# Decode compression of an NSA layer by three products for each pair of compressed rows, with the turning banks emptied by ScalarE

## The chip, the cores and the metric

One Trainium2 chip, one of its cores. The metric is the device time of one execution in microseconds, the median of three runs. All data is fp32.

## The reference, cut to what matters

One decoder layer mixes an HGRN2 head group and an NSA head group, for a prompt of 512 positions and for one new token of each of 8 samples, each with 4096 past positions in 32 pages of 128. For a sample the NSA group computes from its past rows (4 key-value heads of 64 columns):

```
compress(rows, w1, w2, pe), kind k (keys) and v (values):
    sub[n]  = rows[16 n : 16 n + 16]                        # 256 sub-blocks of 16 rows
    h[n]    = const + sub[n] . w1[first half] + sub[n+1] . w1[second half]    # 128 hidden columns
    out[n]  = silu(h[n]) . w2                               # 255 compressed rows
cmp_attention over the 255 compressed rows -> o_cmp and probabilities p
select_blocks(p): the 16 blocks of 64 rows with the highest score (3 of them forced)
selected_attention over the chosen 1024 rows; window_attention over the last 512 rows
out = g0 * o_cmp + g1 * o_slc + g2 * o_win, then the output projection and LayerNorm
```

## The kernel before, in words

hgrn_phase and middle_phase (0 to 1149 us) do the input projection, the HGRN2 group and the whole prompt. decode_output_phase does the decode compression and attention of the 8 samples, then the output projection for all rows (16 tiles of 16 products) and the LayerNorm. The change lies in this last phase, with small edits of the index tables in middle_phase.

**Compression.** GpSimd gathers compressed rows' inputs from the paged cache with indirect DMAs of 128 indices of 2 KB (`rows`, L1481) into X[half], one half of a sample's sub-blocks each (Xr0, and X1, which lies in the old xT): 16 for a half, 32 for a sample. A pass is a pair of kind (keys, values) and half; a sample has four passes. TensorE turns the pass's data (`turn`, L1527, 8 units of four 128x128 transposes into one of two PSUM banks dtb), VectorE empties one half of a bank and ScalarE the other (`empty`, L1754 and L1755, 64x512 each) into XT, and 16 products of 128x128 with 512 columns (`product`, L1550) sum up in one PSUM bank dpH. A pass's turns are made during the pass before it. At a pass's end ScalarE takes the sigmoid (L1804), VectorE the product with it (L1874), and `second` multiplies by w2 into dpK.

**Attention** is cut into pieces, each put by the table PIECES (LAST for the last sample) at a position (g, n) of the passes; `program` makes every engine walk through passes and positions in the same written order, so that an engine that waits in a piece holds back all that stands behind it. The pieces of compressed attention end with the indices gi (L1972) of the chosen rows. Then GpSimd gathers these in four quarters of 8 indirect DMAs (`chosen`, L1497) into the single buffer KV; a quarter is gathered only when the one before has been copied out: `fetch` lets ScalarE copy the keys to Kc (L1830) and VectorE the values to Vg (L1981), `keys` turns Kc (L1650), and so on to the scores, the window's rows and the sum. In GpSimd's own program the gathers of 8 compressed rows for the next sample and a quarter of chosen rows for the sample before alternate:

```
            for p in range(NB + 1):
                for q in range(4):
                    if p + 1 < NB:
                        rows(p + 1, 1 - q // 2, q % 2)
                    if p:
                        chosen(p - 1, q)
```

The passes run on for 9 output tiles (`output`, L1564), so that the last samples' attention lies beside output products. SP loads the window rows and, when X1 and Xr0 are free, the output weights (4 MB each, L1422), then x and the LayerNorm vectors.

## Time and profile before

| | us |
|---|---|
| three runs | 2365.11, 2371.79, 2372.05; median 2371.79 |
| span of the profiled execution, first to last instruction | 2102.9 |
| its own device time | not listed; median less span is 268.9 |
| busy: TensorE / its weight loads | 2062.7 (98%) / 1398.8 (67%) |
| busy: VectorE / ScalarE / GpSimd | 887.5 (42%) / 578.9 (28%) / 628.5 (30%) |

The span is what the hardware profiler saw of the program; the runs' device time has the launch around it. A matmul of fp32 operands appears as two records, a transpose as one. Busy time of DMA-issuing instructions counts on GpSimd (DMA_INDIRECT), where the engine itself makes the descriptors. "idle before" is the engine's idle time just ahead of an instruction, with who ended it; "issue" is idle time for which the profile shows no wait.

### The profile page before, as it was taken

To read this page: it belongs to the slowest core of one execution; us is meant where nothing else is said; L and a number is where in the kernel's file an instruction comes from. 1 tells how busy PE (TensorE), PEld (TensorE's weight loads), DVE (VectorE), ACT (ScalarE), POOL (GpSimd) and SP (SyncE) were. 2 spreads that over 40 slices of the span, in tenths; PEclk is the share of its full clock that TensorE was granted. 3 is DMA by queue.
4 is the path that set the end of the run, shared out by engine and by line. 5 is a ranking of instruction groups with operands and counts; after the bars stand their busy time and mean duration, and the time that the engine had idled before them with its cause. 6 is when DMAs were issued, how large, how long until landed. Compare 5 with 4: busy or idle time off the path is not lost. (4 is left out here: it accounts for less than half of the span.)

```text
span 2102.9 us, 24612 instructions
## 1 busy us (share of the span) xinstructions
PE 2062.7 (98%) x9559; PEld 1398.8 (67%) x9559; DVE 887.5 (42%) x1772; ACT 578.9 (28%) x1067; POOL 628.5 (30%) x675
## 2 busy tenths in 40 slices
PE   8999999999999999999998999999999999899997
PEld 7888888888888887777775555455554555344442
DVE  0354545454531014444445354554545545231227
ACT  0231133113310002322333333434444344200013
POOL 0000000000002003343434537776766765342000
PEclk9999999999999999999998999999999999999998
DMA  5222212222222221111114535566565665643224
GB/s 198 90 80 91 91 71 80 91 91 71 80 82 102 100 87 56 58 43 41 41 41 108 184 112 156 163 192 187 166 197 150 199 195 183 248 129 145 82 80 161
DMA packets 69104, 248.33 MB, mean 118 GB/s; under 512 B 11300, under 2 KB 28912, under 8 KB 57360
## 3 DMA queue, kind: packets, MB, share of 16 engines
q1 hardware_dynamic: 35480, 136.44, 18.6%
q0 software_dynamic: 32256, 106.46, 17.0%
q10 hardware_dynamic: 1280, 4.23, 0.5%
q8 instruction: 59, 0.97, 0.2%
q14 instruction: 29, 0.24, 0.0%
HBM read 226.46 MB, written 20.63 MB: 117 GB/s over the span
## 5 line engine op out<-in xcount | busy, mean ns | idle before, releaser
L292 PE MATMUL pj<-xT,strips 128*128 128x260 f32 x2368 | 532.9, 384 | 6.6 <-DMA xT<-d_xT 6.6
L1550 PE MATMUL dpH<-XT,w 128*128 128x512 f32 x1024 | 505.4, 604 | 0.7 <-DVE XT L1754 0.7
L292 PEld LDWEIGHTS pj<-xT,strips 128*128 128x128 f32 x2368 | 446.2, 191 | 72.5 <-issue 6.6
L1497 POOL DMA_INDIRECT KV<-d_cache,gi x256 | 245.3, 958 | 201.3 <-issue 70.7
L792 PE MATMUL pj<-xT,strips 128*128 128x260 f32 x1216 | 291.0, 387 | 0.0
L792 PEld LDWEIGHTS pj<-xT,strips 128*128 128x128 f32 x1216 | 222.0, 190 | 59.1 <-issue 29.6
L1550 PEld LDWEIGHTS dpH<-XT,w 128*128 128x128 f32 x1024 | 168.2, 190 | 115.7 <-issue 112.5
L1754 DVE COPY XT<-dtb 64x512 f32<-64x512 f32 x256 | 174.8, 683 | 140.2 <-PE dtb L1527 138.7
L1755 ACT ACTIVATE XT<-dtb 64x512 f32<-64x512 f32 x256 | 152.7, 596 | 217.6 <-PE dtb L1527 217.2
L1018 POOL MEMSET kbd<- 128x128 f32 x1 | 0.2, 204 | 635.9 <-POOLq L126 635.9
L1044 POOL TENSOR_SCALAR old<-old,rd 128x128 f32<-128x128 f32 (+3 forms) x116 | 121.9, 1066 | 166.9 <-DVE rd L1153 166.9
L1481 POOL DMA_INDIRECT Xr<-d_cache,row x128 | 121.0, 945 | 53.7 <-issue 38.3
L1481 POOL DMA_INDIRECT xT<-d_cache,row x112 | 106.0, 947 | 51.0 <-issue 33.8
L1564 PE MATMUL dpH<-xT,oT 128*128 128x512 f32 x256 | 118.5, 613 | 0.0
L1564 PE MATMUL dpH<-Xr,oT 128*128 128x512 f32 x256 | 113.1, 596 | 0.0
L1527 PEld LDWEIGHTS dtb<-const,Xr 128*128 128x128 f32 x512 | 62.9, 141 | 70.6 <-issue 59.6
L1527 PEld LDWEIGHTS dtb<-const,xT 128*128 128x128 f32 x512 | 64.7, 143 | 67.0 <-issue 65.4
L1564 PEld LDWEIGHTS dpH<-Xr,oT 128*128 128x128 f32 x256 | 47.6, 190 | 59.8 <-issue 59.6
L1564 PEld LDWEIGHTS dpH<-xT,oT 128*128 128x128 f32 x256 | 48.0, 194 | 56.5 <-issue 56.2
L1170 DVE COPY PT<-mpT 128x512 f32<-128x512 f32 (+2 forms) x48 | 28.9, 602 | 125.3 <-PE mpT L880 125.2
L1527 PE MATMUL dtb<-const,xT 128*128 128x128 f32 x512 | 78.1, 277 | 2.4 <-PEq L126 1.8
L988 ACT ACTIVATE PT<-mpT 128x512 f32<-128x512 f32 (+2 forms) x48 | 25.2, 525 | 199.0 <-PE mpT L880 199.0
(299 smaller groups left out, 2176.6 us busy)
## 6 DMA issues: line engine op xcount, KB each, us to landing
strips<-d_w_in SPq DMA_DIRECT2D x60, 1024.0 KB, 5.1
xT<-d_w_out SPq DMA_DIRECT2D x4, 4096.0 KB, 13.9
d_win_sample<-Wt SPq DMA_DIRECT2D x8, 1024.0 KB, 6.7
Xr<-d_w_out SPq DMA_DIRECT2D x2, 4096.0 KB, 14.6
Wt<-d_win SPq DMA_DIRECT2D x8, 896.0 KB
xT<-d_xT SPq DMA_DIRECT2D x8, 520.0 KB, 9.4
Sold<-d_state SPq DMA_DIRECT2D x8, 512.0 KB, 5.4
vB<-v_rows ACTq DMA_DIRECT2D x8, 512.0 KB, 6.9
```

What stands on the lines that cost most here:

```text
L292: mm = nc.tensor.matmul(pj[b][:, a, 0:TH], w[b][:, k, :], xT[:, k, a * TH:(a + 1) * TH], start=(k == 0), stop=(k == KT - 1))
L792: mm = nc.tensor.matmul(bank(s)[:, n, 0:TH], w[s % 2][:, k, :], xT[:, k, n * TH:(n + 1) * TH], start=(k == 0), stop=(k == KT - 1))
L988: nc.scalar.activation(blocks(brs, 0, qt), pT[:, 0:len(brs) * (qt + 1) * P].rearrange("p (r c n) -> p r c n", r=len(brs), n=P), ACT.Copy). ...
L1044: ins = nc.gpsimd.tensor_scalar(p, p, rd[U % 4][:, k:k + 1], None, ALU.mult)
L1170: V.tensor_copy(blocks(brs, 1, qt), pT[:, 0:len(brs) * (qt + 1) * P].rearrange("p (r c n) -> p r c n", r=len(brs), n=P)).then_inc(pe_v, 1)
L1481: pool.indirect_dma_start(out=X[half][:, r, :], out_offset=None, in_=pairs, in_offset=bass.IndirectOffsetOnAxis(ap=row[:, 2 * b + half, r: ...
L1497: pool.indirect_dma_start(out=KV[0:n, t - 2 * q, h, :], out_offset=None, in_=heads, in_offset=bass.IndirectOffsetOnAxis(ap=gi[b % 2][0:n, ...
L1527: mm = nc.tensor.transpose(tb[bank][:, j * P:(j + 1) * P], X[half][:, 2 * (4 * jg + j) + a, (2 * k + hp) * P:(2 * k + hp + 1) * P], ident)
L1550: mm = nc.tensor.matmul(pH[g % 2][:], w1[:, g % 2, n, :], XT[g % 2][:, jp, :, r:r + HSUB], start=(n == 0), stop=(n == NS - 1))
L1564: mm = nc.tensor.matmul(pH[i % 2][:], oT[:, k, t * P:(t + 1) * P], wo[c % 2][:, k, :], start=(k == 0), stop=(k == KT - 1))
L1754: copy = (lambda d, s: nc.vector.tensor_copy(d, s)) if par == 0 else (lambda d, s: nc.scalar.activation(d, s, ACT.Copy))
L1755: lambda d, s: nc.scalar.activation(d, s, ACT.Copy))
```

## The change

Compressed rows are taken in pairs. With E and O the even and odd sub-blocks, W0 and W1 the two halves of w1: the even output is O.(W0+W1) + (E-O).W0, the odd one O.(W0+W1) + (E'-O).W1, where E' is the next even sub-block. The three products have 512 columns each (128 pairs, 4 heads), so 24 for a kind and 48 for a sample in place of 64. W0+W1 is computed once into ws. To have E and O apart, the index tables gather sub-blocks by parity (X[par]), in quarters of 4 indirect DMAs each (q, of 16 row positions).

The order of work is now counted in slots, one product each: 3 for a step (two of the 32 row positions of w1), 24 for a kind, 48 for a sample. In six slots stand four units of turning (one Q): unit u0 in slot 6Q-7, u1 to u3 in the next three. ScalarE empties each unit's bank with two copies of 64x512 into O and E (Or, D2); VectorE makes E-O and E'-O behind u3 (D1 and D2, four TENSOR_TENSOR of 128x512 for a Q). There are three PSUM banks for the sums; ScalarE copies the common sum to SBUF (`keep_sum`), VectorE adds it to the other two (`join_sum`), then sigmoid (`bend`) and product (`finish`). All banks of keys and window rows that were turned are emptied by VectorE. The tables AT and LAST give the pieces' slots (counted from the sample's first slot); the piece `mix` is what `values` did on TensorE. GpSimd's program now takes all gathers of compressed rows of the next sample, then all four quarters of chosen rows of this one. The output weights are loaded in quarters. The code of `chosen`, and of most attention pieces, is unchanged.

```diff
-        XT = [sb(f"XT{n}", [P, CD // 2, KVH, HSUB + 1]) for n in range(2)]
+        big = sb("big", [P, 16, 512])
+        Or, D1, D2 = (big[:, a:a + 4] for a in (0, 4, 8))
+        ws = big[:, 12:16].rearrange("p a n -> p (a n)").rearrange("p (k j e) -> p k j e", k=2, j=NJ)
...
+        sg = Kc[:].rearrange("p t h d -> p (t h d)")
...
-        pH = [ps(f"dpH{n}", [P, 512]) for n in range(2)]
-        pK, pO = ps("dpK", [P, 512]), ps("dpO", [P, 512])
+        pH = [ps(f"dpH{n}", [P, 512]) for n in range(3)]
+        pK = ps("dpK", [P, 512])
         pS = ps("dpS", [P, 1024])
+        pO = pS[:, 512:768]
...
+        AT = {
+            ("second", 0): 27, ("second", 1): 29, "queries": 25, "scores": 31, "weights": 34, "turned": 36,
+            "sums": 37, "first": 38, "values": 39, "slots": 40, "bases": 41, "rows": 45,
+            ("second", 2): 51, ("second", 3): 53, "fetch0": 54, "keys0": 55, "mix": 56, "acc": 57,
+            "fetch1": 63, "keys1": 64, "fetch2": 70, "keys2": 71, "fetch3": 80, "keys3": 81,
+            "SCORES": 94, "SCALE": 96, "TURNED": 98, "VALUES": 100, "NEWEST0": 106, "NEWEST1": 108,
+            "WSCORES": 109, "WSCALE": 113, "WTURNED": 115, "WVALUES": 116, "SUM": 117, "DONE": 122,
         }
...
+        LAST = {
+            "SCORES": 83, "SCALE": 85, "TURNED": 87, "VALUES": 89, "NEWEST0": 90, "NEWEST1": 91,
+            "WSCORES": 93, "WSCALE": 95, "WTURNED": 97, "WVALUES": 98, "SUM": 99, "DONE": 103,
         }
...
+        UNITS = (1, 0), (1, 1), (0, 0), (0, 1)
...
+        def unit(t):
+            s, n = divmod(t, 3)
+            if s % 2 == 1 and n == 2:
+                Q, u = (s + 3) // 2, 0
+            elif s % 2 == 0:
+                Q, u = s // 2 + 1, n + 1
+            else:
+                return None
+            return (Q, u) if Q < NSTEP // 2 else None
...
+            for s in range(NSTEP):
+                for n in range(3):
+                    do["product"](s, n)
+                    then = unit(3 * s + n)
+                    if then:
+                        do["turn"](*then)
+                    name, which = pieces.get(3 * s + n, (None, None))
+                    if name in do:
+                        do[name](which)
+            for u in range(KT * TILES):
+                i, k = divmod(u, KT)
+                do["output"](i, k)
+                name, which = pieces.get(3 * NSTEP + u, (None, None))
+                if name in do:
+                    do[name](which)
+                if k == KT - 1:
+                    do["end"](i)
...
-                sp.dma_start(wo[n][:], io["w_out"][c]).then_inc(wo_in[n], 16)
-            def read(b, g):
-                for u in (6, 7):
-                    bank, k = place[(g, b, u)]
-                    sp.wait_ge(tr[bank], k + 1)
-            for b in range(NB - 2):
+                for a in range(4):
+                    if i < 2:
+                        bank, k = place[NSTEP // 2 - 4 + a, 1 + 2 * n]
+                        sp.wait_ge(tr[bank], k + 1)
+                    sp.dma_start(wo[n][:, 4 * a:4 * a + 4], io["w_out"][c][:, 4 * a:4 * a + 4]).then_inc(wo_in[n][a], 16)
+            for b in range(NB - 1):
                 window(b)
-            read(NB - 1, 1)
             weights(0)
-            window(NB - 2)
-            read(NB - 1, 3)
             weights(1)
-            for n in range(2):
-                sp.wait_ge(hid[n], 2 * NB)
+            sp.wait_ge(prod, NSTEP)
+            sp.wait_ge(hs_r, 4 * NB)
             for t in range(NQT):
                 sp.dma_start(z[t], io["x"][t * P:(t + 1) * P]).then_inc(z_in, 16)
...
-            def rows(b, half, part):
-                if b and part == 0:
-                    for u in (6, 7):
-                        bank, k = place[(3 - 2 * half, b - 1, u)]
-                        pool.wait_ge(tr[bank], k + 1)
-                for r in range(8 * part, 8 * part + 8):
+            def rows(b, q, par):
+                if b:
+                    bank, k = place[NJ * b - 4 + q, 3 - 2 * par]
+                    pool.wait_ge(tr[bank], k + 1)
+                for r in range(4 * q, 4 * q + 4):
                     pool.indirect_dma_start(
-                        out=X[half][:, r, :], out_offset=None, in_=pairs,
-                        in_offset=bass.IndirectOffsetOnAxis(ap=row[:, 2 * b + half, r:r + 1], axis=0),
-                    ).then_inc(x_in[half][part], 16)
+                        out=X[par][:, r, :], out_offset=None, in_=pairs,
+                        in_offset=bass.IndirectOffsetOnAxis(ap=row[:, 2 * b + par, r:r + 1], axis=0),
+                    ).then_inc(x_in[par][q], 16)
...
-            rows(0, 0, 0)
-            rows(0, 0, 1)
-            for p in range(NB + 1):
+            for q in range(4):
+                rows(0, q, 0)
+            for p in range(NB):
+                if p + 1 < NB:
+                    for q in range(4):
+                        rows(p + 1, q, 1)
+                        rows(p + 1, q, 0)
                 for q in range(4):
-                    if p + 1 < NB:
-                        rows(p + 1, 1 - q // 2, q % 2)
-                    if p:
...
-            def turn(g, b, u):
-                k, half = g % 2, half_of(g)
-                a, hp, jg = u % 2, u // 2 % 2, u // 4
-                if u % 4 == 0:
-                    pe.wait_ge(x_in[half][jg], 128 * b + 128)
-                bank = free((g, b, u))
-                for j in range(4):
-                    mm = nc.tensor.transpose(tb[bank][:, j * P:(j + 1) * P],
-                                             X[half][:, 2 * (4 * jg + j) + a, (2 * k + hp) * P:(2 * k + hp + 1) * P],
-                                             ident)
+            def turn(Q, u):
+                m, q = divmod(Q, 4)
+                b, kind = divmod(m, 2)
+                par, a = UNITS[u]
+                if kind == 0 and a == 0:
+                    pe.wait_ge(x_in[par][q], 64 * (b + 1))
+                bank = free((Q, u))
+                for i in range(4):
+                    r, hp = 4 * q + 2 * (i // 2) + a, i % 2
+                    mm = nc.tensor.transpose(tb[bank][:, i * P:(i + 1) * P],
+                                             X[par][:, r, (2 * kind + hp) * P:(2 * kind + hp + 1) * P], ident)
                 mm.then_inc(tr[bank], 1)
-            def product(p, g, n):
-                if p >= NB:
-                    output(4 * (p - NB) + g, n)
-                    return
+            def product(s, n):
+                m, j = divmod(s, NJ)
+                kind = m % 2
+                if s == 0 and n == 0:
+                    pe.wait_ge(ws_r, 1)
+                    pe.wait_ge(init, 6)
+                if s == 0 and n == 2:
+                    pe.wait_ge(gp_r, 1)
                 if n == 0:
-                    if (p, g) == (0, 1):
-                        pe.wait_ge(gp_r, 1)
-                        pe.wait_ge(init, 7)
-                    for u in (6, 7):
-                        bank, k = place[(g, p, u)]
-                        pe.wait_ge(ev[bank], emptied[(g, p, u)][1])
-                    if g >= 2:
-                        for a in range(2):
-                            pe.wait_ge(edge[a], 2 * p + g - 1)
-                    need(pe, hs_r[g % 2], 2 * p + g // 2)
-                r, jp = divmod(n, CD // 2)
-                if (p, g, n) == (0, 0, CD // 2):
-                    pe.wait_ge(seam, 2)
-                mm = nc.tensor.matmul(pH[g % 2][:], w1[:, g % 2, n, :], XT[g % 2][:, jp, :, r:r + HSUB],
-                                      start=(n == 0), stop=(n == NS - 1))
-                if n == NS - 1:
-                    mm.then_inc(hid[g % 2], 1)
+                    turned_in((s // 2, 1))
+                    if j == 0:
+                        need(pe, kept, m)
+                else:
+                    pe.wait_ge(diff_r, 2 * s + n)
+                    if j == 0:
+                        need(pe, added, 2 * m - 2 + n)
+                left = (ws[:, kind, j], w1[:, kind, j], w1[:, kind, NJ + j])[n]
+                right = (Or, D1, D2)[n][:, s % 4]
+                mm = nc.tensor.matmul(pH[n][:], left, right, start=(j == 0), stop=(j == NJ - 1))
+                if n == 2:
+                    mm.then_inc(prod, 1)
+                elif j == NJ - 1:
+                    mm.then_inc(full[n], 1)
             def output(i, k):
...
+            def turn(Q, u):
+                bank, k = place[Q, u]
+                par, a = UNITS[u]
+                act.wait_ge(tr[bank], k + 1)
+                need(act, prod, 2 * Q - 2)
+                dst = (D2, Or)[par][a * DH:(a + 1) * DH, 2 * (Q % 2):2 * (Q % 2) + 2].rearrange(
+                    "p j (h b n) -> p j h b n", h=2, b=2)
+                for hd in range(2):
+                    ins = A(dst[:, :, :, hd], tb[bank][hd * DH:(hd + 1) * DH].rearrange(
+                        "p (j h n) -> p j h n", j=2, h=2), ACT.Copy)
+                ins.then_inc(ev[bank], 1)
+            def keep_sum(m):
+                act.wait_ge(full[0], m + 1)
+                need(act, k2, 2 * m)
+                A(hs[1].rearrange("p a n -> p (a n)"), pH[0][:], ACT.Copy).then_inc(kept, 1)
+            def bend(m, par):
+                act.wait_ge(added, 2 * m + par + 1)
+                need(act, hs_r, 2 * m + par)
+                if keyed[0]:
+                    bank, k = place[keyed[0]]
+                    act.wait_ge(tr[bank], k + 1)
+                A(sg, hs[par].rearrange("p a n -> p (a n)"), ACT.Sigmoid,
+                  bias=hb[:, m % 2:m % 2 + 1]).then_inc(bent, 1)
+                bends[0] = 2 * m + par + 1
+            def product(s, n):
+                m, j = divmod(s, NJ)
+                if (j, n) == (NJ - 1, 0):
+                    keep_sum(m)
+                if (j, n) == (NJ - 1, 2):
+                    bend(m, 0)
+                if (j, n) == (0, 0) and m:
+                    bend(m - 1, 1)
+            def output(i, k):
+                if (i, k) == (0, 0):
+                    bend(2 * NB - 1, 1)
...
                         act.wait_ge(tr[bank], k + 1)
+                    need(act, hs_r, bends[0])
+                    keyed[0] = QUARTERS[q], b
                     A(Kc[:], KV[:, :, :, 0:DH], ACT.Copy).then_inc(k_c, 1)
...
+            def differences(Q):
+                bank = place[Q, 3][0]
+                v.wait_ge(ev[bank], emptied[Q, 3][1])
+                need(v, prod, 2 * Q - 2)
+                for s in (2 * Q % 4, 2 * Q % 4 + 1):
+                    V.tensor_tensor(D1[:, s], D2[:, s], Or[:, s], ALU.subtract).then_inc(diff_r, 1)
+                    e, o = (t[:, s].rearrange("p (h n) -> p h n", h=KVH) for t in (D2, Or))
+                    v.wait_ge(diff_r, 4 * Q + 2 * (s % 2) + 1)
+                    V.tensor_tensor(e[:, :, 0:HSUB - 1], e[:, :, 1:HSUB], o[:, :, 0:HSUB - 1],
+                                    ALU.subtract).then_inc(diff_r, 1)
+            def turn(Q, u):
+                if u == 3:
+                    differences(Q)
+            def join_sum(m, par):
+                v.wait_ge(kept, m + 1)
+                if par == 0:
+                    v.wait_ge(full[1], m + 1)
+                else:
+                    v.wait_ge(prod, NJ * (m + 1))
+                need(v, k2, 2 * (m - 1) + par + 1)
+                V.tensor_tensor(hs[par].rearrange("p a n -> p (a n)"), pH[1 + par][:],
+                                hs[1].rearrange("p a n -> p (a n)"), ALU.add).then_inc(added, 1)
+            def finish(m, par):
+                v.wait_ge(bent, 2 * m + par + 1)
+                h = hs[par].rearrange("p a n -> p (a n)")
+                V.scalar_tensor_tensor(h, h, hb[:, m % 2:m % 2 + 1], sg, ALU.add, ALU.mult).then_inc(hs_r, 1)
+            def product(s, n):
+                m, j = divmod(s, NJ)
+                if j == NJ - 1 and n:
+                    join_sum(m, n - 1)
+                if j == 0 and n < 2 and m:
+                    finish(m - 1, n)
+            def output(i, k):
+                if i == 0 and k < 2:
+                    finish(2 * NB - 1, k)
             def second(which):
-                g, b = which
```

## Rows read from the trace of the kernel before

**Rows 1.** Busy time by engine in one stretch: us, engines (instructions), granted clock, DMA share, GB/s
```profile
1400.00:1450.00 50.00, 49.88 (x223) 25.45 (x221) 27.55 (x62) 23.17 (x37) 35.05 (x37) 1.00 0.55 163
```
**Rows 2.** Timeline of TensorE: start us, us, engine, line, operation, out<-in, count
```profile
1166.89 7.89 PE L1550 MATMUL dpH<-XT,w 128*128 128x512 f32 x18
1500.54 1.02 PE L1550 MATMUL dpH<-XT,w 128*128 128x512 f32 x2
1501.84 1.02 PE L1550 MATMUL dpH<-XT,w 128*128 128x512 f32 x2
```
**Rows 3.** Products of the compression and of the output: durations, first and last start
```profile
L1550 PE MATMUL dpH<-XT,w x1024: 592/592/697, 1156.4 to 1819.0; 128*128 128x512 f32 x171
L1564 PE MATMUL dpH<-xT,oT x256: 592/592/1221, 1819.5 to 2020.0; 128*128 128x512 f32 x128
```
**Rows 4.** Groups by line, GpSimd, 1148 to 1960 us: busy us, mean ns | idle before
```profile
L1497 POOL DMA_INDIRECT KV<-d_cache,gi x256 | 245.3, 958 | 201.3 <-issue 70.7 <-ACT Kc L1830 57.8 <-DVE Vg L1981 56.3
L1481 POOL DMA_INDIRECT Xr<-d_cache,row x128 | 121.0, 945 | 53.7 <-issue 38.3 <-PE dtb L1527 15.4
```
**Rows 5.** Timeline of GpSimd: the gathers of chosen rows that waited, over one sample
```profile
1427.13 0.94 POOL L1497 DMA_INDIRECT KV<-d_cache,gi  x1 [1.20 <-ACT Kc L1830]
1450.98 0.94 POOL L1497 DMA_INDIRECT KV<-d_cache,gi  x1 [4.06 <-DVE Vg L1981]
1472.36 0.94 POOL L1497 DMA_INDIRECT KV<-d_cache,gi  x1 [1.52 <-ACT Kc L1830]
1513.41 0.94 POOL L1497 DMA_INDIRECT KV<-d_cache,gi  x1 [1.20 <-ACT Kc L1830]
```
**Rows 6.** Timelines of GpSimd and ScalarE near the end: gathers and copies of Kc
```profile
1814.10 0.94 POOL L1497 DMA_INDIRECT KV<-d_cache,gi  x1 [8.19 <-ACT Kc L1830]
1918.41 0.94 POOL L1497 DMA_INDIRECT KV<-d_cache,gi  x1 [8.74 <-ACT Kc L1830]
1812.69 0.63 ACT L1830 ACTIVATE Kc<-KV 128x512 f32<-128x512 f32 x1 [8.50 <-DMA KV<-d_cache,gi]
1929.69 0.63 ACT L1830 ACTIVATE Kc<-KV 128x512 f32<-128x512 f32 x1 [12.06 <-DMA KV<-d_cache,gi]
```
**Rows 7.** Groups by line, VectorE and ScalarE, 1148 to 1960 us
```profile
L1754 DVE COPY XT<-dtb 64x512 f32<-64x512 f32 x256 | 174.8, 683 | 140.2 <-PE dtb L1527 138.7
L1755 ACT ACTIVATE XT<-dtb 64x512 f32<-64x512 f32 x256 | 152.7, 596 | 217.6 <-PE dtb L1527 217.2
L1953 DVE TENSOR_TENSOR pg<-const,idxf 4x1024 f32<-4x1024 f32 x8 | 9.7, 1212 | 0.3
L2036 DVE TENSOR_TENSOR om<-om,acc 16x256 f32<-16x256 f32 x7 | 2.9, 413 | 0.2
```
**Rows 8.** Timelines of VectorE and GpSimd: gathers beside a subtraction-like instruction
```profile
1323.98 1.21 DVE L1953 TENSOR_TENSOR pg<-const,idxf 4x1024 f32<-4x1024 f32 x1
1324.22 1.79 POOL L1497 DMA_INDIRECT KV<-d_cache,gi  x1 [0.30 <-issue]
1496.54 1.21 DVE L1953 TENSOR_TENSOR pg<-const,idxf 4x1024 f32<-4x1024 f32 x1
1497.34 1.20 POOL L1497 DMA_INDIRECT KV<-d_cache,gi  x1 [0.30 <-issue]
```
**Rows 9.** TensorE around its longest wait of the stage (timeline), and a window after it
```profile
1837.63 1.12 PE L1650 MATMUL dtb<-const,Kc 128*128 128x128 f32 x4 [7.80 <-ACT Kc L1830]
1838.54 1.92 PE L1564 MATMUL dpH<-xT,oT 128*128 128x512 f32 x2
1844.00:1846.00 2.00, 2.00 (x4) 0.67 (x2) 1.83 (x8) 0.00 (x0) 1.39 (x3) 0.50 0.93 380
```
**Rows 10.** Timeline of GpSimd at the start: first gather, a late one, first chosen rows
```profile
1149.73 0.95 POOL L1481 DMA_INDIRECT Xr<-d_cache,row  x1 [0.21 <-issue]
1241.45 0.94 POOL L1481 DMA_INDIRECT xT<-d_cache,row  x1 [17.19 <-PE dtb L1527]
1259.44 0.94 POOL L1497 DMA_INDIRECT KV<-d_cache,gi  x1 [8.18 <-DVE gi L1972]
```

273 lines of the change are left out of this document (107 added, 166 removed).

## The prediction

> **What bounds the kernel now.** I read the stages first. In the decode stage (1156 to 1819 us) a stretch of 50 us shows TensorE busy for 49.88 of it at the full granted clock, VectorE for 27.6, ScalarE for 23.2, and GpSimd for 35.1 us with 37 instructions [rows 1]. TensorE's own sequence confirms it: nine products of 512 columns (18 records) in a row take 7.89 us, one alone 1.02 with its drain, so one beside its neighbours (7.89 - 1.02)/8 = 0.86 us; from product to product with a turn of four transposes between them it is 1.30, so a turn takes 0.44 [rows 2]. The 1024 product records run from 1156.4 to 1819.0 [rows 3]. TensorE is the bound, and the change takes a quarter of its products away.
>
> The second engine is the one to look at. GpSimd's busy time hides 0.30 us ahead of every gather: its DMA_INDIRECTs follow each other at 1.25 us, whichever tile they fill (0.945 to 0.958 busy and 0.30 "issue") [rows 4]. Each decode sample needs 32 gathers of compressed rows and 32 of chosen rows, that is 64 x 1.255 = 80.3 us. The sample's period is read between the same gather of two samples: 1427.13 to 1513.41, 86.3 us [rows 5]. GpSimd is thus occupied for 93% of the time with TensorE at 100%. It waits 1.20, 4.06 and 1.52 us in a period [rows 5], because 8 gathers of compressed rows stand between one quarter of chosen rows and the next, and hide that quarter's landing.
>
> **TensorE's part.** The period splits into 64 products x 0.86 = 55.0, 32 turns x 0.44 = 14.1, and the rest, 17.2 us, for the attention pieces. After: 48 x 0.86 = 41.3, the same 32 turns (8 groups of 4 units for each sample) and pieces: 72.6 us. Gain 13.7 us for each sample, 110 over eight. It counts only if nobody else needs over 72.6.
>
> **GpSimd's part.** The number of gathers does not change (4 per quarter and parity, x 8; 8 per chosen quarter, x 4), so 80.3 us stay, and that alone leaves at most 6 of the 13.7. But the order changes: all 32 gathers of compressed rows, then the four quarters of chosen rows back to back. KV is one buffer; quarter q+1 is issued only after ScalarE and VectorE have copied quarter q out. In the tail of the old kernel, where nothing stands between, the price is seen: first issue at 1918.41, copy of Kc at 1929.69 (11.3 us), and from a copy's start (1812.69) to the next issue (1814.10) 1.4 us [rows 6]. So 12.7 us from quarter to quarter where 8 x 1.26 = 10.1 are issues: 2.6 us x 3 = 7.9 us. Floor of the new period 40.0 + 40.3 + 7.9 = 88.2 us.
>
> **The subtractions and the port.** VectorE loses 32 copies of 0.683 us for each sample [rows 7] and gets 32 subtractions of 128x512, both operands in SBUF. The trace has such an operation at 1024 and 256 elements, 1212 and 413 ns [rows 7]; in between, 512 cost 0.68 us. So VectorE's load stays. But GpSimd is held up by them: a gather that starts at 1324.22, while the TENSOR_TENSOR with both operands in SBUF runs (1323.98 to 1325.19), takes 1.79 in place of 0.95 us; one at 1497.34 against 1496.54 to 1497.75 takes 1.20 [rows 8]. Both fit one reading: some 0.13 us after its start the gather needs something which VectorE holds, and waits till that instruction ends. Four subtractions in a row (2.9 us) catch about 1.8 gathers at 0.34 us each, 0.6 us; 8 groups x 0.6, less GpSimd's idle share, and four longer instructions at the end of the hidden layer: 4.5 us a sample. Bounds: nothing, and every gather hit once by a mean of 0.34, 22 us. I take 4.5, counted from the overlap. The Trainium skill's page "SBUF — State Buffer" (The single rule, in the section on who interferes with whom) says that a VectorE instruction with two SBUF inputs contends with a GpSimd one that reads SBUF, but infers that descriptor generation is spared, as it needs only the write side. The two stretched gathers speak for the first sentence and against the second; by the second the term would be 0.
>
> **The emptying by ScalarE alone.** 64 copies of 0.596 us [rows 7] for each sample are 38 us, twice as before; with sigmoids, exponentials, table loads and Kc some 56 us. Below every period here, so nothing in the mean. In a run of four turns ScalarE needs 2 x 0.60 = 1.2 us against TensorE's 1.30 for each: it just keeps up, except where a sigmoid falls into the run or ScalarE waits for an exponential's maximum; I give TensorE 6 us of stalls a sample for this (bounds 0 and 12), which lie beside GpSimd's time in the steady stage and count once, in the last stretch.
>
> **The path from quarter 0 to quarter 1.** Fetch 0 stands at slot 54 (48 slots, one product each, for a sample), fetch 1 at 63, and VectorE has to do the subtractions of slot 62 before its copy. From the copy of Kc: keys0 1.4, seven products 6.0, five turns 2.2, the mix 1.1, ScalarE 1.2, subtractions 3.0, Vg 0.4: 15.3 us, then the issue at 15.6, where GpSimd alone would be ready at 14.1. 1.5 us more.
>
> **The clock.** From fetch 2 (slot 70) TensorE needs 32 slots, about 50 to 57 us, to the next keys0; GpSimd needs 10 + 40 + 9.7 + 1.6 + 4 = 65. So TensorE idles 8 to 14 us in every sample, inside ScalarE's wait. The trace shows what an idle time of 7.80 us does: work resumes at 1837.63 with two records at 1.92 in place of 1.02 us, and at 1844 to 1846 the granted clock is still 0.50, 1.2 GHz [rows 9]; I reckon with 9 us from the resumption. 9 us at half rate do 4.5 us of work. They fall just on the path from quarter 0 to quarter 1. Bounds 0 and 4.5; I take 4.0.
>
> **The sum.** Period 88.2 + 4.5 + 1.5 + 4.0 = 98.2 us, 11.9 above before.
> - Start: the first products come about 3 us later than 1156.4 [rows 3], as the first units need rows of the other parity, whose gathers start at 1149.73 [rows 10]. A slot without pieces is (6 x 0.86 + 4 x 0.44)/6 = 1.15 us; GpSimd resumes with sample 1 when slot 18 is turned, 1159.4 + 19 x 1.15 = 1181 (before it still waits for a buffer at 1241.45 [rows 10]). Then 40 + 4 us of gathers, chosen rows of sample 0 from 1226, against 1259.44 before [rows 10]; its quarter 3 at 1226 + 3 x 12.7 + 1.5 = 1265.6.
> - Six periods: quarter 3 of sample 6 at 1854.8, slot 358 at 1853.4.
> - To slot 384, the end of products: 26 x 0.86 + 12 turns x 0.44 + pieces 6.1 + stalls 6 = 39.8: 1893.2, where before has 1819.5 [rows 3]. +73.7.
> - Tail: the same 256 output products. Some pieces (the compressed scores of sample 7, the chosen scores of 6) are already done: -4. The 7.80 us stall [rows 9] is a late landing behind the output weights and x rows just issued; the new loads come in quarters but meet the last gathers likewise: unchanged. The output waits of SP for single banks cost nothing, they precede use by over 20 us.
>
> Sum +69.7. The profiled execution has a span of 2102.9 us; its own device time isn't listed, so I set the 268.9 us to the median of 2371.8 as what lies around it, unchanged: **2441 us**.
>
> **Rivals.**
> 1. *TensorE stays the bound*, the gain is whole: -110, 2262 us. For it: 98% busy. Against: GpSimd would need 64 gathers in 72.6 - 7.9 us, 1.01 us each, where the rows show 1.25 without exception. It decides below 1.01 us. Chance 0.07.
> 2. *GpSimd bounds, with the landings hidden*: period 80.3, six of them 107 us less than mine, with a start 6 us earlier: 2328 us. Against: the serial quarters of rows 6. Chance 0.05.
> 3. *Floor only*: landings cost, port, path and clock nothing. Period 88.2: quarter 3 of sample 6 at 1788, products end at 1821, 2369 us. The later period is paid by the earlier start. Chance 0.12.
> 4. *The gathers need nothing of what the subtractions hold*: 6 x 4.5 + 4 less, 2410 us; or *the clock is held* through the idle times: 24 less, 2417. Chance 0.12 and 0.13. (The skill's inference quoted above would make the first of them.)
> 5. *ScalarE falls behind as well*, and its backlog joins the path at each fetch: 6 x 7 more, 2483 us. Chance 0.11.
> That the products aren't fewer is excluded by the code.
>
> **How the numbers follow.** The forecast has 0.40. Within 0.3% of the median, 7 us, is about what a measurement of this kernel can tell from no change. Faster: rivals 1 and 2 and a third of 3, 0.16; same: half of 3, 0.06; slower: all else, 0.78. The range holds the forecast, 4, most of 3 and half of 5: 2366 to 2482.
>
> **What would show it.** GpSimd still at 1.25 us a gather, with "ACT Kc" or "DVE Vg" waits of 2.5 us and more ahead of three quarters in four; more of its instructions above 1.0 us (now nearly all 0.95), with subtractions beside them; idle TensorE of 8 to 14 us before the transposes of Kc once a sample and a granted clock of 0.5 behind it; the period between like gathers 94 to 100 us. TensorE at 100% through the stage and a period of 73 us would prove me wrong, and so would GpSimd issuing other work between chosen quarters.

## The result, and the profile after

| | us |
|---|---|
| before, four runs | 2365.11 to 2372.05, median 2371.55 |
| changed kernel, four runs | 2324.08 to 2333.39, median 2328.65 |
| ratio, 95% interval | 0.9822 [0.9804, 0.9841]: 1.8% faster |
| forecast | 2441, range 2366 to 2482 |

The forecast missed on the wrong side. The profile after, its page (span, busy time, share of the chain, groups):

```profile
span 2326.8 us, 24655 instructions
PE 2027.1 (87%) x9303; PEld 1374.4 (59%) x9303; DVE 913.9 (39%) x1813; ACT 707.9 (30%) x1289; POOL 643.2 (28%) x673
...
PE 21%; DVE 7%; another core or an unknown queue 7%; ACT 6%; issue 5%; POOL 2%; DMA 2%; ACTq 1%; DVEq 0%; POOLq 0%
...
L1799 ACT ACTIVATE big<-dtb 64x512 f32<-64x512 f32 x512 | 302.4, 591 | 403.6 <-PE dtb L1534 185.4
L1501 POOL DMA_INDIRECT KV<-d_cache,gi x256 | 249.1, 973 | 341.6 <-ACT Kc L1856 121.9
...
L1900 DVE TENSOR_TENSOR big<-big 128x512 f32<-128x512 f32 x128 | 88.1, 688 | 188.6 <-ACT big L1799 125.7
```

The operations have the durations that the sum used: the copies 591 ns against 596, the subtractions 688 against my 680. But the span is 2326.8 of 2328.65 us: only 1.9 us lie around it, where I had set 268.9. And GpSimd's waits show a period (1476.22 to 1596.19, quarter 0 to quarter 0) of 120.0 us, 119.6 as the mean of the four from 1356.52 to 1835.09, where the profile of before has 86.3 [rows 5] and I had forecast 98.2. Timeline of GpSimd, the gathers of chosen rows that waited:

```profile
1476.22 0.94 POOL L1501 DMA_INDIRECT KV<-d_cache,gi  x1 [6.51 <-DVE gi L2030]
1497.17 0.94 POOL L1501 DMA_INDIRECT KV<-d_cache,gi  x1 [11.25 <-ACT Kc L1856]
1516.47 0.94 POOL L1501 DMA_INDIRECT KV<-d_cache,gi  x1 [9.35 <-DVE Vg L2039]
1533.43 0.95 POOL L1501 DMA_INDIRECT KV<-d_cache,gi  x1 [7.25 <-ACT Kc L1856]
1596.19 0.94 POOL L1501 DMA_INDIRECT KV<-d_cache,gi  x1 [6.45 <-DVE gi L2030]
```

So the slower period is there, and yet the kernel is faster than before. Against the profile of before its span is 224 us longer, against the runs of before its time is 43 us shorter. Both can only hold if the execution of before that was profiled isn't like those that were timed. The chain also has a share that before's profile has not: "another core or an unknown queue". In the list of waits it is "remote", and it falls into the row gathers of each sample. Four timelines of one such place (ScalarE, VectorE, TensorE and GpSimd):

```profile
1565.88 1.20 ACT L1799 ACTIVATE big<-dtb 64x512 f32<-64x512 f32 x2 [24.60 <-remote]
...
1549.76 0.43 DVE L1940 COPY kcT<-dpK 128x256 f32<-128x256 f32 x1 [5.00 <-remote]
1567.32 0.43 DVE L1940 COPY kcT<-dpK 128x256 f32<-128x256 f32 x1 [17.13 <-remote]
...
1544.87 0.66 PE L1534 MATMUL dtb<-const,xT 128*128 128x128 f32 x4 [0.62 <-DVEq L2107]
1550.33 1.12 PE L1602 MATMUL dpK<-hs,w2v 128*64 128x256 f32 x4 [4.81 <-issue]
1567.13 1.11 PE L1534 MATMUL dtb<-const,Xr 128*128 128x128 f32 x4 [12.05 <-ACT big L1799]
...
1567.63 0.94 POOL L1485 DMA_INDIRECT xT<-d_cache,row  x1 [4.64 <-remote]
```

TensorE's transposes end at 1545.53, and ScalarE, which waits for nothing else, copies them out at 1565.88. The product by w2 ends at 1551.45, VectorE copies it at 1567.32. In the other direction nothing is late: TensorE starts 0.05 us after ScalarE's copy. I call this a **held signal**: a semaphore that TensorE raises, acted on by the waiting engine up to 20 us later. The trace has only both ends of it; whether the signal is late or the waiting engine is late to act on it, no run tells. GpSimd issues 24 gathers without a break from 1533.43 to 1563. The long waits end 3 to 5 us after it stops, one of VectorE (5.00 us) already at 1549.76, in the middle of the run. And what stops GpSimd there is a wait for TensorE of the same kind, its own 4.64 us. Waits of the kind, from 1250 us on:

```profile
ACT big L1799 <- remote: 161.3, 21, 24.6
DVE kcT L1940 <- remote: 112.4, 11, 20.6
```

### The profile page after: what moved, and what is told of

Same layout as the page of the kernel before. It is cut to its first block, busy times and chain, and to the rows that moved or that the text cites. A ratio compares the mean times of both kernels' runs of the same rounds, so it can differ in the third digit from the quotient of the medians.

```text
span 2326.8 us, 24655 instructions
## 1 busy us (share of the span) xinstructions
PE 2027.1 (87%) x9303; PEld 1374.4 (59%) x9303; DVE 913.9 (39%) x1813; ACT 707.9 (30%) x1289; POOL 643.2 (28%) x673
## 4 chain that ended last, share of the span: by engine, by line
PE 21%; DVE 7%; another core or an unknown queue 7%; ACT 6%; issue 5%; POOL 2%; DMA 2%; ACTq 1%; DVEq 0%; POOLq 0%
PE dpH L1575 9%; PE dpH L1557 6%; ACT big L1799 4%; PE dtb L1534 3%; POOL KV L1501 2%; DVE big L1900 2%; DMA KV<-d_cache,gi 2%; DVE big L1903 1%; PE dtb L1662 1%; ACTq L1813 1%; PE dpS L1613 1%; ACT Kc L1856 1%; PE dpS L1712 0%; PE dpK L1607 0%
## 5 line engine op out<-in xcount | busy, mean ns | idle before, releaser
L1799 ACT ACTIVATE big<-dtb 64x512 f32<-64x512 f32 x512 | 302.4, 591 | 403.6 <-PE dtb L1534 185.4
L1557 PE MATMUL dpH<-big,w 128*128 128x512 f32 x512 | 284.8, 653 | 0.6 <-DVE hs L1917 0.4
L1534 PE MATMUL dtb<-const,Xr 128*128 128x128 f32 x512 | 86.9, 298 | 90.5 <-issue 50.6
L1900 DVE TENSOR_TENSOR big<-big 128x512 f32<-128x512 f32 x128 | 88.1, 688 | 188.6 <-ACT big L1799 125.7
L1557 PE MATMUL dpH<-big 128*128 128x512 f32 x256 | 147.3, 660 | 0.0
L1485 POOL DMA_INDIRECT Xr<-d_cache,row x128 | 131.9, 1030 | 46.8 <-issue 39.0
L1557 PEld LDWEIGHTS dpH<-big,w 128*128 128x128 f32 x512 | 89.3, 205 | 63.1 <-issue 51.8
L1534 PE MATMUL dtb<-const,xT 128*128 128x128 f32 x512 | 84.1, 290 | 28.5 <-DVE KgT L1771 16.4
L1662 PE MATMUL dtb<-const,Kc 128*128 128x128 f32 (+1 forms) x128 | 27.5, 327 | 89.6 <-ACT Kc L1856 88.5
L1903 DVE TENSOR_TENSOR big<-big 128x508 f32<-128x508 f32 x128 | 88.3, 690 | 4.4
```

Of the source, the lines that this page charges most:

```text
L1485: pool.indirect_dma_start(out=X[par][:, r, :], out_offset=None, in_=pairs, in_offset=bass.IndirectOffsetOnAxis(ap=row[:, 2 * b + par, r:r ...
L1534: mm = nc.tensor.transpose(tb[bank][:, i * P:(i + 1) * P], X[par][:, r, (2 * kind + hp) * P:(2 * kind + hp + 1) * P], ident)
L1557: mm = nc.tensor.matmul(pH[n][:], left, right, start=(j == 0), stop=(j == NJ - 1))
L1662: mm = nc.tensor.transpose(tb[bank][:, j * P:j * P + n], Kc[0:n, t, 2 * hp:2 * hp + 2, :].rearrange("p h d -> p (h d)"), ident[0:n, 0:n])
L1799: ins = A(dst[:, :, :, hd], tb[bank][hd * DH:(hd + 1) * DH].rearrange("p (j h n) -> p j h n", j=2, h=2), ACT.Copy)
L1900: V.tensor_tensor(D1[:, s], D2[:, s], Or[:, s], ALU.subtract).then_inc(diff_r, 1)
```

## The experiments

"The occasion" below is a set of kernels measured side by side with the kernel before. All times are medians; the ratio is to before on the same occasion. From e9 on the first kernel of an occasion has its time of before in bold. e3 to e7 do less work or compute from part of the rows.

| kernel | us | before beside it | ratio, 95% interval |
|---|---|---|---|
| e1 before | 2371.36 | 2367.80 | 1.0011 [0.9995, 1.0028] |
| e2 interleaved | 2359.52 | 2367.80 | 0.9954 [0.9936, 0.9972] |
| e3 changed, no row gathers | 2203.28 | 2367.80 | 0.9302 [0.9263, 0.9340] |
| e4 before, no row gathers | 2125.92 | 2367.80 | 0.8975 [0.8941, 0.9010] |
| e5 before, 256 B rows | 2368.83 | 2370.10 | 0.9994 [0.9971, 1.0017] |
| e6 changed, 256 B rows | 2337.71 | 2370.10 | 0.9887 [0.9852, 0.9922] |
| e7 changed, 1 KB rows | 2340.17 | 2370.10 | 0.9889 [0.9849, 0.9929] |
| e8 changed, fours | 2358.87 | 2370.10 | 0.9959 [0.9940, 0.9978] |
| e9 changed, lagged wait | 2192.27 | **2102.01** | 1.0430 [1.0409, 1.0451] |
| e10 before, gaps | 2200.52 | 2102.01 | 1.0468 [1.0451, 1.0486] |
| e11 changed, gaps | 2280.29 | 2102.01 | 1.0848 [1.0830, 1.0866] |
| e12 before, MEMSETs | 2101.79 | 2102.01 | 0.9999 [0.9990, 1.0009] |
| e13 changed, as it is | 2189.71 | **2102.73** | 1.0413 [1.0396, 1.0430] |
| e14 as e12 | 2102.25 | 2102.73 | 0.9998 [0.9988, 1.0007] |
| e15 as e10 | 2203.13 | **2102.47** | 1.0471 [1.0454, 1.0488] |
| e16 as e2 | 2291.08 | 2102.47 | 1.0892 [1.0873, 1.0910] |
| e17 table and order | 2343.30 | **2371.91** | 0.9878 [0.9844, 0.9912] |
| e18 table alone | 2373.61 | 2371.91 | 1.0011 [0.9992, 1.0029] |

**Where are the 268.9 us?** e1 is the kernel before as it is.

> The kernel before, unchanged: it asks where 268.9 us of its device time (2371.8) lie, as the profiled execution had a span of only 2102.9, while the changed kernel shows 2326.8 of 2328.65 in the span. Theory A (my prediction's reading: launch around the span): span 2103, device time 2371. Theory B (the execution profiled before was not like the timed ones, and the timed ones hold the same stalls that the changed kernel shows, 'another core or an unknown queue' in the burst of row gathers, about 20 us a sample): spans within 3 us of the device time, about 2369, and a fresh profile has such stalls, 150 us or more in sum. Theory C (a lower granted clock in the timed executions): spans about 2369 with a mean granted clock well below that of the first profile.

Its span is 2369.5 us. Its page (groups) and one run of gathers (timelines of ScalarE, VectorE, TensorE, GpSimd):

```profile
span 2369.5 us, 24612 instructions
...
L1754 DVE COPY XT<-dtb 64x512 f32<-64x512 f32 x256 | 174.8, 683 | 358.2 <-remote 234.4
...
L1755 ACT ACTIVATE XT<-dtb 64x512 f32<-64x512 f32 x256 | 152.7, 596 | 477.1 <-remote 314.9
...
1499.94 0.59 ACT L1755 ACTIVATE XT<-dtb 64x512 f32<-64x512 f32 x1 [7.17 <-remote]
1499.94 0.68 DVE L1754 COPY XT<-dtb 64x512 f32<-64x512 f32 x1 [7.08 <-remote]
...
1493.00 0.63 PE L1527 MATMUL dtb<-const,xT 128*128 128x128 f32 x4 [1.04 <-DVE XT L1754]
1500.68 1.11 PE L1527 MATMUL dtb<-const,xT 128*128 128x128 f32 x4 [6.19 <-DVE XT L1754]
...
1479.34 0.94 POOL L1497 DMA_INDIRECT KV<-d_cache,gi  x1 [12.69 <-ACT Kc L1830]
1489.34 0.95 POOL L1481 DMA_INDIRECT Xr<-d_cache,row  x1 [0.30 <-issue]
1498.09 0.95 POOL L1481 DMA_INDIRECT Xr<-d_cache,row  x1 [0.30 <-issue]
```

And two windows of it (busy time of TensorE, its weight loads, VectorE, ScalarE, GpSimd; granted clock; DMA share; GB/s):

```profile
1489.00:1494.50 5.50, 4.46 (x22) 2.35 (x20) 0.87 (x3) 0.60 (x1) 3.98 (x6) 1.00 0.60 175
1502.60:1505.00 2.40, 2.40 (x6) 0.84 (x7) 1.78 (x4) 2.35 (x4) 0.00 (x0) 0.50 0.00 0
```

Theory B holds. The copies' durations are those of rows 7 to the nanosecond; their idle time is not. Transposes that end at 1493.63 are copied out at 1499.94, by both engines at the same instant, at the end of a run of 16 gathers (8 of chosen, 8 of compressed rows, 1479 to 1499). The first period is 118.6 us (chosen rows first at 1294.43, same quarter at 1413.01), the mean of five (to 1920.35) is 125.2, 38.9 above the 86.3 of rows 5. Theory C has a share in it: with the same instructions TensorE is busy for 2145.2 us against 2062.7, and the mean granted clock is 0.949 against 0.990. The rows show where: TensorE stands idle for 6.19 us before 1500.68, and then works at a granted clock of 0.50, 1.2 GHz, to 1505. So of the 266.6 us between the two spans some 184 are idle time of TensorE and some 82 slower work.

**Which gathers hold the signals?** e3 and e4 leave out the row gathers of samples 1 to 7, which are then computed from sample 0's rows:

```diff
-                if p + 1 < NB:
-                    for q in range(4):
-                        rows(p + 1, q, 1)
-                        rows(p + 1, q, 0)
...
-                    pe.wait_ge(x_in[par][q], 64 * (b + 1))
+                    pe.wait_ge(x_in[par][q], 64)
```

> The changed kernel without the gathers of compressed rows for samples 1 to 7 (every sample is computed from the rows of sample 0; the rest of the work stays). Theory A (the once-a-sample stall of ScalarE and VectorE sits in the burst of row gathers): no such stall is left, period near TensorE's own 73 to 80 us, device time 2328 - 7 x 42 = 2035 (2000 to 2060). Theory B (the stall comes from something else that recurs each sample, like loading of instructions): the period stays above 95 us, device time above 2150.

> The kernel before without the gathers of compressed rows for samples 1 to 7 (samples computed from the rows of sample 0). If its timed executions are bound by TensorE as its first profile shows (period 86.3 us): little changes, within 1% of the 2371 of before. If its timed executions hold stalls tied to the row gathers (268.9 us over 7 periods is 38 us each): 2371 - 7 x 38 = 2105, a period near 86.

e4 falls by 242 us to 2125.9, 21 above what was expected for stalls tied to the row gathers, and from 1380 us on TensorE is busy for 86.79 of 87.00 us. ScalarE's waits of the kind fall from 314.9 to 31.8 us, 14.5 of them before 1180 us, beside the gathers of sample 0, which stay. The other 17.3 are six waits of up to 3.5 us, and they stand at the end of runs of 8 gathers of chosen rows. One of them (TensorE, ScalarE, first and last gather of the run):

```profile
1477.23 0.60 PE L1525 MATMUL dtb<-const,xT 128*128 128x128 f32 x4
1479.80 1.22 ACT L1753 ACTIVATE XT<-dtb 64x512 f32<-64x512 f32 x2 [3.29 <-remote]
...
1468.37 0.94 POOL L1497 DMA_INDIRECT KV<-d_cache,gi  x1 [14.35 <-DVE Vg L1979]
1477.29 0.95 POOL L1497 DMA_INDIRECT KV<-d_cache,gi  x1 [0.30 <-issue]
```

So a run of 8 can hold a signal too, here for 2.0 us (1477.83 to 1479.80). e3 refutes the 2035 of its theory A: the stalls all but go (ScalarE's waits of the kind are 6.1 us from 1250 us on), but the period stays, 99.5 us twice and 101.6 as the mean of six (1279.18 to 1888.62). I come back to that.

e5, e6 and e7 keep every gather and cut its bytes (e7: 256 columns in place of 64; e5 in `rows` of before likewise). Samples 1 to 7 then get only part of their rows:

```diff
+                n = 2 * KVH * DH if b == 0 else 64
...
-                        out=X[par][:, r, :], out_offset=None, in_=pairs,
+                        out=X[par][:, r, 0:n], out_offset=None, in_=cache.rearrange("g r (s d) -> (g r s) d", d=n),
```

> The kernel before; for samples 1 to 7 each gather of compressed rows brings 256 bytes per index in place of 2 KB (the rest of the rows stays that of sample 0). GpSimd's 64 gathers a sample stay, only the bytes go. Theory A (the 'remote' waits for TensorE's signals come from the bytes that the row gathers move): they go, period 86.3 us as in the first profile, device time 2371 - 7 x 32 = 2145 or a little less (2105 to 2150). Theory B (they come with any GpSimd gather, whatever its size): unchanged, 2371 within 1%.

> The changed kernel with the same edit: 256 bytes per index for the compressed rows of samples 1 to 7. Here the model of my prediction (GpSimd bound, chosen quarters back to back) is on trial without the stalls: period 98.2 us. Theory A (bytes make the stalls, the model is right otherwise): period 98 to 101, device time 2328 - 7 x 20 = 2190 (2175 to 2210), thus slower than the kernel before with the same edit by 45 to 75 us. Theory B (stalls from any gather): 2328 within 1%.

> The changed kernel with 1 KB per index for the compressed rows of samples 1 to 7: half the bytes. Theory A1 (the stall grows with the bytes): half of what the 256-byte variant saves, about 2260. Theory A2 (a threshold: below some rate the signals pass): as the 256-byte variant, about 2190.

Bytes are not the cause: an eighth of them leaves 2368.8 and 2337.7 us, theory B of both. e7's 2340.2 is neither of its two.

e8 makes GpSimd wait after every four row gathers until they have landed, with the same work:

```diff
                     ).then_inc(x_in[par][q], 16)
+                pool.wait_ge(x_in[par][q], 64 * (b + 1))
```

> The changed kernel; GpSimd waits after every 4 row gathers until they have landed, so that never more than 4 are under way. Same work. It costs GpSimd 8 waits of about 2.5 us a sample, 20 us. Theory A3 (the stall is a backlog of transfers that builds up in the burst): stalls fall to a few us each, at most 8 us a sample; period about 110 to 114, device time 2270 to 2300. Theory A4 (a single row gather in flight is enough to hold the signals): stalls stay in sum near 20 us and GpSimd's waits come on top: 2370 to 2450.

Its timelines of GpSimd and ScalarE tell more than its time:

```profile
1311.72 1.07 POOL L1485 DMA_INDIRECT xT<-d_cache,row  x1 [0.30 <-issue]
1315.61 0.95 POOL L1485 DMA_INDIRECT xT<-d_cache,row  x1 [0.30 <-issue]
1319.57 0.95 POOL L1485 DMA_INDIRECT Xr<-d_cache,row  x1 [3.02 <-DMA xT<-d_cache,row]
1327.29 1.07 POOL L1485 DMA_INDIRECT xT<-d_cache,row  x1 [3.02 <-DMA Xr<-d_cache,row]
...
1316.65 1.20 ACT L1800 ACTIVATE big<-dtb 64x512 f32<-64x512 f32 x2 [7.46 <-remote]
```

After 1250 us held signals are left in one place of each sample: where quarter 3 and the first four row gathers make a run of 12 (to 1316.6). None falls on a run of 4 with the 3.02 us of waiting behind it, nor, in this kernel, on a quarter of 8 by itself. So here the length of GpSimd's unbroken run decides; at gaps of 1 to 2 us (e6 and e17 have such runs) signals are still held. ScalarE's waits of the kind fall from 161.3 to 54.5 us, but GpSimd's waits for landings of rows come to 145.5 us, and the 2358.9 lie between the ranges of both theories.

e2 changes the order of the gathers:

```diff
+            for p in range(NB):
+                chosen(p, 0)
+                chosen(p, 1)
+                both(p + 2, 0)
+                chosen(p, 2)
+                both(p + 2, 1)
+                chosen(p, 3)
+                both(p + 2, 2)
+                both(p + 2, 3)
```

> The changed kernel, but GpSimd's order alternates as before: quarters 0 and 1 of the chosen rows, 8 row gathers of the next sample, quarter 2, 8 row gathers, quarter 3, 16 row gathers. Same work. Theory A (the stall of about 20 us a sample comes from 32 large row gathers, 256 KB each, in one burst, behind which other transfers queue): stalls shrink to under 8 us a sample, and the period falls from 119.6 to about 100 to 105, device time about 2328 - 7 x 15 = 2220. Theory B (the chosen quarters that nothing hides are the price, the stalls are not tied to the burst): two of three landings hidden, 5 us a sample, 2290. Theory C (neither, GpSimd is not on the path any more): 2328 within 0.5%.

It is slower than the changed kernel, by 31 us. The order was badly chosen: the rows of `both(p + 2, 0)` may come only when TensorE has turned slot 66, and the fetch at slot 70 needs quarter 2, now queued behind them. Theory A wasn't tested by it.

**The same kernel at 2102 us.** The next three occasions turned out to be of another kind: the median of before was 2102.0, 2102.7 and 2102.5 us (33 runs), and the profiles have no wait of the kind at all. One chip, by its number, showed both times. e9, e11, e10 and e12 had been meant to break the runs of gathers; here there was nothing to mend, and they show the price of the means.

```diff
# e9: wait for the landing of the group of four but one before
+                if len(under_way) > 1:
+                    pool.wait_ge(*under_way.pop(0))
...
+                under_way.append((x_in[par][q], 64 * (b + 1)))
# e10, e11, e15: wait for the landing of the last 8 gathers
+            def landed(now):
+                if last:
+                    pool.wait_ge(*last.pop())
+                last.append(now)
# e12, e14: behind every four gathers
+                nc.gpsimd.memset(pad[:], 0.0).then_inc(brk, 1)
```

> The changed kernel; before each group of 4 row gathers GpSimd waits for the landing of the group but one before it, so at most 8 row gathers are under way, with hardly a pause if they land 3.7 us after issue. Same work. Theory P (TensorE's signals are held while GpSimd issues over 8 to 12 gathers without a pause, and let go when it pauses): no pause, so the stalls stay at 15 us and more, device time 2328 within 1%. Theory Q (they are held by a backlog of gathers under way): the wait bounds the backlog, stalls fall below 5 us, device time 2250 to 2300.

> The kernel before; GpSimd waits ahead of every group of 8 gathers (rows or chosen) until the group before it has landed, so no run of gathers is longer than 8. Same work. Theories P and Q alike: no held signals; GpSimd has 64 x 1.255 = 80.3 us plus 4 more landings of 2.6 us and the natural waits, period 92 to 97 us in place of 118.6, device time 2371 - 7 x 24 = 2200 (2170 to 2230). Rival (the runs of 16 aren't what holds the signals): the landings come on top, 2371 to 2440.

> The changed kernel with the same edit: no run of gathers over 8. GpSimd's floor 88.2 us plus 4 more landings of 2.6 us = 98.6, and the variant without any row gathers has a period of 100 to 106, so the period is 103 to 110 in place of 119.6: 2328 - 7 x 13 = 2237 (2210 to 2270). By this the changed kernel is slower than the kernel before once neither has the stall, by some 40 us, which is what I had predicted without knowing of the stall (+70). Rival (runs of gathers aren't what holds the signals): 2328 to 2420.

> The kernel before; after every 4 gathers GpSimd does a MEMSET of 128x16 in a scratch tile (about 0.2 us), with no wait for landings. Same work otherwise. Theory P1 (any other instruction on GpSimd between gathers is pause enough): stalls gone, period 88 to 92 us, device time 2371 - 7 x 29 = 2170 (2140 to 2190). Theory P2 (the pause has to be a real idle time of a us or more, or the landings count): 2371 to 2400, stalls as before.

In e10 GpSimd waits ahead of each of the eight groups of a sample, mostly 2 to 3 us, where before it waited three times [rows 5]. This costs before 98 us, (2200.5 - 2102.0)/7 = 14.1 a sample, 1.8 for each of the eight waits, and the changed kernel about 13 a sample (2280.3 - 2189.7 = 90.6 over 7). The lagged wait of e9 costs it 2.6 us. The MEMSETs cost nothing. Whether any of them lets held signals through, no run shows: e10's 2200 lies in the range of its expectation (2170 to 2230) by luck, as no signal was held in before beside it.

e13 is the changed kernel as it is, e14 repeats e12.

> The changed kernel, unchanged. The kernel before has shown two times on different occasions, about 2370 us (signals of TensorE held for 4 to 8 us in each run of 16 gathers) and 2102 us (none held; the execution profiled first is of this kind). If before takes 2102 beside it: my forecast goes by that profile, so the changed kernel should take 2102 + 70 = 2172 us with a period of 98.2 us and no 'remote' waits; the variant with a wait for the landing of the group but one before, already seen at 2192 with a period near 101, is an upper bound. Rival: above 2192, period over 101. If before takes 2370 beside it: 2328 again, period 119.6, stalls of 20 us a sample.

> The kernel before with a MEMSET of 128x16 on GpSimd after every 4 gathers. If before takes 2102 beside it: 2102 again. If before takes 2370: Theory P1 (any other instruction between gathers lets the held signals through): 2140 to 2190, period 88 to 92 us; Theory P2 (it takes real idle time of GpSimd, or landings): 2370 to 2400, with ScalarE and VectorE waiting 4 to 8 us in each run of 16 gathers.

**2189.7 us, 4.1% slower than before**, where the forecast's own sum from a profile of this kind gives 2102.9 + 69.7 = 2172.6 of span, and the span is 2188.1. One period of e13, and two short windows in it (windows; groups of GpSimd with its waits; TensorE's longest waits for Kc):

```profile
1337.40:1437.30 99.90, 81.11 (x341) 40.34 (x341) 48.09 (x105) 51.69 (x85) 62.33 (x64) 0.93 0.54 155
1371.50:1373.50 2.00, 1.97 (x6) 1.32 (x7) 1.07 (x2) 0.75 (x1) 0.94 (x2) 0.50 1.03 426
1377.50:1379.50 2.00, 1.60 (x11) 0.98 (x9) 0.33 (x3) 1.94 (x4) 1.55 (x2) 1.00 0.37 123
...
L1501 POOL DMA_INDIRECT KV<-d_cache,gi x32 | 30.5, 953 | 27.4 <-ACT Kc L1856 10.0 <-issue 8.8 <-DVE Vg L2039 8.6
L1485 POOL DMA_INDIRECT Xr<-d_cache,row x16 | 16.1, 1008 | 4.9 <-issue 4.6 <-PE dtb L1534 0.3
L1485 POOL DMA_INDIRECT xT<-d_cache,row x16 | 15.7, 982 | 4.9 <-issue 4.9
...
1353.28 0.66 PE L1662 MATMUL dtb<-const,Kc 128*128 128x128 f32 x4 [1.08 <-ACT Kc L1856]
1371.53 1.11 PE L1662 MATMUL dtb<-const,Kc 128*128 128x128 f32 x4 [6.20 <-ACT Kc L1856]
1392.76 0.99 PE L1662 MATMUL dtb<-const,Kc 128*128 128x128 f32 x4 [2.15 <-ACT Kc L1856]
```

And the same of e3, the changed kernel without row gathers:

```profile
1419.80:1519.30 99.50, 79.07 (x342) 39.31 (x340) 47.88 (x105) 51.67 (x84) 30.90 (x33) 0.95 0.25 71
...
1458.66 0.66 PE L1658 MATMUL dtb<-const,Kc 128*128 128x128 f32 x4 [1.08 <-ACT Kc L1852]
1476.94 1.12 PE L1658 MATMUL dtb<-const,Kc 128*128 128x128 f32 x4 [6.24 <-ACT Kc L1852]
1498.19 0.99 PE L1658 MATMUL dtb<-const,Kc 128*128 128x128 f32 x4 [2.15 <-ACT Kc L1852]
...
1519.26 0.95 POOL L1501 DMA_INDIRECT KV<-d_cache,gi  x1 [32.05 <-DVE gi L2026]
```

This is the pair to read. TensorE's waits for Kc are the same to 0.04 us with 64 gathers a sample and with 32, and in e3 GpSimd idles for 32.05 us ahead of quarter 0. (e3 was measured where before takes 2368 us, but these 99.5 us of it have no held signal.) So the row gathers don't set the period of 99.9. What does is argued from the waits, as no run leaves out the chosen rows: their quarters follow each other through one buffer, and TensorE's transposes of them stand at fixed places in its program. It waits 10.1 us for Kc and some 9 us elsewhere in a period, at a granted clock of 0.93. The row gathers just fit: GpSimd's ledger is 62.3 busy + 18.3 issue + 18.9 waits.

e15 repeats e10, e16 repeats e2, beside before at 2102.

> The kernel before, with GpSimd waiting ahead of every group of 8 gathers for the landing of the group before it (no run over 8). If before takes 2102 beside it: 2200 again, as seen (only the landings' price). If before takes 2370: by the theory that TensorE's signals are held in runs of over 8 gathers, this kernel doesn't mind: 2200 (2190 to 2220), no 'remote' waits over 2 us in the decode stage; rival (the runs aren't the cause): 2400 and more.

> The changed kernel with the row gathers put between the quarters of chosen rows (quarters 0 and 1, 8 row gathers, quarter 2, 8, quarter 3, 16). If before takes 2102: the changed kernel's GpSimd waited 18.9 us in a period of 99.9 (3.8, 8.5 and 6.6 ahead of three quarters). Theory A (these back-to-back quarters are what costs): two of the three waits go, period 84 to 90, device time 2190 - 7 x 12 = 2106 (2090 to 2130). Theory B (GpSimd's waits are only its slack, TensorE's order of pieces sets the period): within 1% of 2190. If before takes 2370: 2359 as seen.

e16's 2291 us are 101 above the changed kernel and refute both theories. GpSimd now waits for TensorE in turn (timeline):

```profile
1476.94 0.94 POOL L1501 DMA_INDIRECT KV<-d_cache,gi  x1 [13.64 <-ACT Kc L1865]
1498.05 0.94 POOL L1485 DMA_INDIRECT xT<-d_cache,row  x1 [10.56 <-PE dtb L1543]
```

e2 and e16 are one kernel at both times, 2359.5 and 2291.1 us: what the held signals cost it is 68 us.

The fetches' places in the table of pieces belong to the order of the gathers. e17 moves both, e18 the table alone.

```diff
-            "fetch1": 63, "keys1": 64, "fetch2": 70, "keys2": 71, "fetch3": 80, "keys3": 81,
+            "fetch1": 66, "keys1": 70, "fetch2": 80, "keys2": 81, "fetch3": 91, "keys3": 92,
# fetch0 57, keys0 59, acc 62; the last sample keeps its places. e17 alone:
+                chosen(p, 0)
+                both(p + 1, 3)
+                for q in range(3):
+                    chosen(p, q + 1)
+                    both(p + 2, q)
```

> The changed kernel with GpSimd's order alternating one group later than before (quarter 0, last 8 rows of the next sample, quarter 1, first 8 rows of the next but one, quarter 2, 8, quarter 3, 8) and the table moved to it: fetch0 57, fetch1 66, fetch2 80, fetch3 91 in place of 54, 63, 70, 80. Same work. If before takes 2102: Theory A (the serial quarters, for GpSimd and for TensorE's fixed places of the fetches alike, are the price of the change): hardly any wait is left, the period is set by GpSimd's 82 us and falls from 99.9 to 84 to 88, device time 2190 - 7 x 13.5 = 2095 (2080 to 2120), level with or a little below before's 2102. Theory B (something else in the change, like ScalarE's single-handed emptying, holds the period near 100): 2170 or more. If before takes 2370: runs of 16 gathers as before, signals held, 2300 to 2330.

> The changed kernel with the moved table alone (fetch0 57, fetch1 66, fetch2 80, fetch3 91), GpSimd's order as in the changed kernel. If before takes 2102: Theory A: the four quarters still stand back to back and now wait for later fetches (9, 14 and 11 slots of some 1.6 us), so GpSimd's row gathers start later: period 100 to 110, 2190 to 2260. Theory C (TensorE's stall at the old places of the fetches is the price, not GpSimd's order): period under 93, 2140 or less. If before takes 2370: 2328 to 2400.

Before took 2371.9 us beside them, signals were held again (174.2 us of ScalarE's waits in e17, in runs of 16 to 24), and the question of the 4.1% wasn't answered. e17 misses its 2300 to 2330 by 13 us. Later fetches alone cost 45 us against the changed kernel (2373.6 and 2328.65, on two occasions), so the fetches' places do reach the end; the alternating order takes 30 of them back (e17 against e18, side by side). What either would do at 2102 was not seen.

## Why the prediction was wrong, and where it was right

**The step that failed first** is the last of the sum: "I set the 268.9 us to the median of 2371.8 as what lies around it, unchanged". What lies around the span is 1.8 to 2.0 us in every run whose span is on record. The 268.9 us were time inside the decode stage that the profiled execution didn't have: products end at 1819.5 there [rows 3] and at 2085.4 in e1, 265.9 us later. The changed kernel has them end at 1920.8 (e13) and at 2059.8, 139.0 later. So the held signals cost before 266 us and the changed kernel 139, and -1.8% is the difference of a loss of 87 us, which the change costs where no signals are held, and a gain of some 127 us that no part of my sum held. By samples: 125.2 - 86.3 = 38.9 us in before, over four runs of 16 gathers; 119.6 - 99.9 = 19.7 in the changed kernel, mostly over one run of 24. Why it pays half as much isn't shown. The order of the gathers alone isn't the reason: the alternating order of e2 and e16 pays 68 us. Where no signals are held, TensorE is busy for 98% of the span in before and for 92% in the changed kernel; a late signal may cost less where it waits anyway. That is argued.

A gap of 11% between span and device time, where the page itself shows no wait to fill it, should have been a rival with a chance. The profile could not tell what it was, but any one timed run with its span would have told that 268.9 us is no launch. Rival 2 has the number that came, 2328 us against 2328.65, and that is chance: it wanted the landings hidden and a period of 80.3 us, while GpSimd waited 7.25 to 11.25 us ahead of three of its quarters, in a period of 120.

**Against before at 2102 us the sum can be judged term by term.**
- Start: products from 1161.4 (forecast 1159.4), GpSimd resumes at 1184.7 (1181), chosen rows from 1228.2 (1226), quarter 3 of sample 0 at 1270.9 (1265.6). Right, 5 us short.
- Six periods: 603.0 us to quarter 3 of sample 6 at 1873.95, 100.5 each (forecast 98.2). Near, but for another reason. "GpSimd bounds" was wrong: e3 has 99.5 without half of its gathers. Its ledger (99.5 us) and the period that e3 has without the row gathers come out at nearly the same length.
- Port: gathers are stretched beside the subtractions, 1008 and 982 ns against 945 [rows 4]; in a period 62.3 us busy against 60.9 before, 1.4 us where I took 4.5: the term is a third of mine. The Trainium skill's page "SBUF — State Buffer" (Who interferes with whom) says that a VectorE instruction with two SBUF inputs contends with a GpSimd one that reads SBUF. The trace of e13 agrees: a gather at 1413.04, over three subtractions, takes 1.31 us. The page's inference that descriptor generation is spared isn't borne out.
- Landings, path and clock, 7.9 + 1.5 + 4.0 = 13.4 forecast: GpSimd's waits are 18.9.
- TensorE: I expected one idle time of 8 to 14 us before the transposes of Kc. It is 10.1, but in four waits, the longest 6.20 (with others 18.8 in all). Behind that one the granted clock is 0.50 at 1371.5 to 1375.5 and 1.00 from 1377.5, so it is low for some 5 us where I reckoned with 9. The mechanism is there and smaller than I took it.
- ScalarE alone: TensorE waits for its copies 2.0 us a period, against 6 allowed. Rival 5 fell.
- End: output products start 46.8 us after quarter 3 of sample 6 (38.4 forecast, 1854.8 to 1893.2), and the tail is 267.3 us against 283.4 before, -16 where I took -4.

In sum +85.2 us of span for +69.7. I had 5 us too little at the start, 14 in the periods and 8 up to the output products, and the tail gave back 12 more than I took: in part the sum comes near because errors cancel. Rival 1, TensorE bound and 110 us gained, is refuted at both times: its share of busy time falls from 98% to 92% (e13) and 87%.

**What stays open.** Why the same kernel takes 2102 us at one time and 2370 at another. What a held signal is in the machine, and whether the waiting engines are held up by something else, such as late instructions: nothing was run on it. Whether a short MEMSET or gaps between runs of 8 free them: the variants ran only where none were held. And which of order and places makes the 4.1%. No version here that does the whole work beats both kernels: the changed one is the fastest where before takes 2370 us, before (with or without MEMSETs) where it takes 2102.

## What to carry to other kernels

Compare the span of a profile with the timed runs before building on it; if they differ by more than a few us, the profile is of another kind of execution, and a forecast from it needs a chance for "something else fills the gap". An engine that looks like the bound by its load can be tested by leaving half of its load out: if the other engines' waits stay the same to hundredths, it isn't. And an order of gathers is one thing with the table of places where they are consumed: here each of them moved alone cost time (e2 and e16, e18).

## What the runs showed of the hardware

- In unbroken runs of indirect gathers on GpSimd, waits of ScalarE, VectorE and GpSimd for TensorE ended up to 20 us late, while TensorE's own wait ended promptly (0.05 us). Such waits were up to 24.6 us long in runs of 12 to 28 gathers (e1, the changed kernel, e8), up to 3.5 us at the end of some runs of 8 (e4), and there was none in runs of 4 with 3.02 us between them (e8), whatever the bytes of each gather (256 B or 2 KB per index). And only at some times: 2370 against 2102 us for one kernel, seen on one chip.
- Behind 6.2 us of idle time TensorE's granted clock was 0.50 for some 4 to 5 us (e1, e13).
- A wait of GpSimd for its last 4 gathers to land took about 3 us (3.02 in e8). Eight such waits a sample, for 8 gathers each, cost 14.1 us of device time where GpSimd is nearly full (e10).
- A MEMSET of 128x16 behind every four gathers, 16 a sample, cost nothing (0.9999 and 0.9998); its 0.14 us fell into the 0.30 us between two gathers.
